# The gates' one-hot products of an expert layer in the rounded format, with the weight split in two halves side by side

## The reference

```python
sc, idx = lax.top_k(s, PEER_TOPK)
cand = (sc[:, :, 0, :, None] + sc[:, :, 1, None, :]).reshape(T, PEER_HEADS, PEER_TOPK * PEER_TOPK)
cidx = (idx[:, :, 0, :, None] * PEER_NKEYS + idx[:, :, 1, None, :]).reshape(T, PEER_HEADS, PEER_TOPK * PEER_TOPK)
top_sc, pos = lax.top_k(cand, PEER_TOPK)
eidx = jnp.take_along_axis(cidx, pos, axis=-1)
gate = jax.nn.softmax(top_sc.astype(jnp.float32), axis=-1).astype(h.dtype)
...
    act = jax.nn.gelu(jnp.einsum('thkd,td->thk', u_tab[eb], hb), approximate=False)
    return jnp.einsum('thk,thkd->td', gb * act, v_tab[eb])
```

## Time and profile before

| | us |
|---|---|
| median of 3 runs | 3858.21 (3856.76 to 3859.42) |
| the profiled execution | 3858.48 |
| its span from first to last instruction | 3856.7 |
| PE busy | 3712.3 (96%) |
| DVE busy | 2270.4 (59%) |
| POOL busy | 1402.2 (36%) |
| ACT busy | 1327.3 (34%) |
| chain that ended last: PE, all lines | 92% |
| of it the gate products, L578 | 3% |
| granted TensorE clock, mean | 0.979 |

### The profile page before, as it was taken

One profiled execution on the slowest core, in us unless ns is written; L12 is line 12 of the kernel. 1 busy time (PEld: TensorE's weight loads), 2 busy tenths in 40 slices (PEclk: granted clock), 3 DMA queues, 4 the chain that ended last, 5 costly groups with the idle time before them and its releaser, 6 DMA issues.

```text
span 3856.7 us, 48588 instructions
## 1 busy us (share of the span) xinstructions
PE 3712.3 (96%) x16460; PEld 2917.3 (76%) x16460; DVE 2270.4 (59%) x3639; ACT 1327.3 (34%) x1826; POOL 1402.2 (36%) x596
## 2 busy tenths in 40 slices
PE   6999899899999999999999999999999999999998
PEld 4787787688888888878888887854688877358886
DVE  5786996145767585167777775335574431657441
ACT  4554323334443434321111113246322232653221
POOL 2211443333333333344444443410244444124442
PEclk8999999999999999999999999989999999899999
DMA  5435222233546464676556652221132223212232
GB/s 200 148 109 195 95 92 78 88 94 111 177 146 188 136 191 134 213 250 187 183 183 186 187 180 95 94 66 43 55 98 93 98 89 96 64 43 93 96 96 77
DMA packets 266641, 486.58 MB, mean 126 GB/s; under 512 B 16721, under 2 KB 148177, under 8 KB 266097
## 3 DMA queue, kind: packets, MB, share of 16 engines
q1 hardware_dynamic: 81936, 299.93, 24.6%
q10 hardware_dynamic: 184580, 184.95, 14.8%
HBM read 415.48 MB, written 84.02 MB: 130 GB/s over the span
## 4 chain that ended last, share of the span: by engine, by line
PE 92%; DVE 3%; ACT 2%; issue 1%; DMA 1%; POOL 0%; DVEq 0%; SPq 0%; ACTq 0%; POOLq 0%
PE ps L356 26%; PE ps L358 26%; PE ps L357 26%; PE ps L578 3%; PE ps L653 3%; PE ps L671 2%; DMA ring<-panels 1%; PE ps L661 1%; PE ps L453 1%; PE ps L389 1%; PE ps L558 0%; PE ps L384 0%; DVE sq L1368 0%; DVE arena L1468 0%; PE ps L464 0%
## 5 line engine op out<-in xcount | busy, mean ns | idle before, releaser
L1967 POOL TENSOR_TENSOR ring_r<-ring,high_w 128x1024 fp32r<-128x1024 f32 x552 | 1366.0, 2476 | 2240.3 <-ACT high_w L770 1757.6
L356 PE MATMUL ps<-uT_r,high_w 128*128 128x512 f32 x2624 | 1047.9, 399 | 23.2 <-POOL ring_r L1967 10.2
L358 PE MATMUL ps<-uT_r,ring_r 128*128 128x512 f32 x2624 | 1028.2, 392 | 0.0
L770 ACT ACTIVATE high_w<-ring 128x1024 fp32r<-128x1024 f32 x440 | 464.4, 1058 | 1283.4 <-PE ps L358 1134.4
L357 PE MATMUL ps<-sq_r,high_w 128*128 128x512 f32 x2048 | 800.0, 391 | 0.0
L357 PE MATMUL ps<-part,high_w 128*128 128x512 f32 x1856 | 735.0, 396 | 0.0
L356 PE MATMUL ps<-part,high_w 128*128 128x512 f32 x1664 | 670.1, 403 | 11.6 <-issue 7.1
L358 PE MATMUL ps<-part,ring_r 128*128 128x512 f32 x1664 | 658.6, 396 | 0.0
L356 PEld LDWEIGHTS ps<-uT_r,high_w 128*128 128x128 f32 x2624 | 497.6, 190 | 131.3 <-issue 19.9
L358 PEld LDWEIGHTS ps<-uT_r,ring_r 128*128 128x128 f32 x2624 | 496.6, 189 | 104.8
L357 PEld LDWEIGHTS ps<-sq_r,high_w 128*128 128x128 f32 x2048 | 386.7, 189 | 79.8 <-issue 1.9
(11 more groups left out here) (288 smaller groups left out, 3770.5 us busy)
## 6 DMA issues: line engine op xcount, KB each, us to landing
ring<-panels SPq DMA_DIRECT2D x568, 512.0 KB, 3.5
gdram<-arena ACTq DMA_DIRECT2D x16, 2048.0 KB, 10.6
arena<-gdram ACTq DMA_DIRECT2D x128, 256.0 KB, 5.3
arena<-adram ACTq DMA_DIRECT2D x128, 256.0 KB, 2.7
adram<-act_out ACTq DMA_DIRECT2D x112, 256.0 KB, 3.9
arena<-ada_rest ACTq DMA_DIRECT2D x32, 512.0 KB, 4.5
strips_dram<-btab ACTq DMA_DIRECT2D x4, 3584.0 KB
arena<-strips_dram ACTq DMA_DIRECT2D x32, 448.0 KB, 3.3
```

The source lines that it names most:

```text
L356: t_.matmul(out, wh, xh, start=(k == 0), stop=False)
L358: last = t_.matmul(out, wl, xh, start=False, stop=(k == KT - 1))
L770: s_.activation(high_w[:, j % RING], ring[:, j % RING], ACT.Copy).then_inc(hi_ready, 1)
L1967: g_.tensor_tensor(ring_r[:, j], ring[:, j], high_w[:, j], ALU.subtract).then_inc(lo_ready, 1)
```

## The change

The four products of a group go to the rounded format. A one-hot is exact in it, the weight is not, so the weight is cut into a high half (rounded) and a low half (what is left). The moving operand then is, per token, two blocks of 128 columns: onehot(a) x high and onehot(a) x low. The product has 256 columns and yields two partial gates, and their sum is the gate. The pieces:

- after L569, DVE copies the transposed keys from PSUM into `slot` in SBUF (L1732 of the changed kernel) and forms the two halves of the weight in `slotT` (L1733, L1734), once per token tile;
- `hot`: one comparison of 1024 elements writes the one-hots of both keys of four tokens (`hots`, in `st`, L1741), one multiplication of 1024 elements writes the two halves (`halves`, in the work area's tile `rest`, L1742). All their inputs are in SBUF;
- PE: four products of 256 columns instead of four plain ones of 128, into two banks per group, 4 to 7 in turn;
- ACT copies the high partial gates into `gbuf` as before, 512 elements;
- `gate_sum`: DVE adds the low partial gates from PSUM to `gbuf`, in place (L1750), 512 elements with the same 512-byte step;
- PE waits for that sum (`g_sum`) where it waited for ACT's copy (`g_evac`), and ahead of the transposes of the next tile. DVE writes the one-hots of two groups ahead of the loop, and then alternates `hot` of the next round with `gate_sum` of this one.

```diff
                 pe.wait_ge(slot_ready, 3 * (tt + 1))
+                pe.wait_ge(g_sum, 32 * tt + 2)
...
                             pe.wait_ge(hot_ready, n * 1 + 1)
-                            pe.wait_ge(g_evac, n * 1 + 1)
+                            pe.wait_ge(g_sum, n * 1 + 1)
                             for k in range(4):
-                                last = t_.matmul(ps[:, 6 + par, k * P:(k + 1) * P], brng[:, 4 * par + k, :],
-                                                 arng[:, 4 * par + k, :], start=True, stop=True)
+                                last = t_.matmul(ps[:, 4 + 2 * par + k // 2, 2 * P * (k % 2):2 * P * (k % 2 + 1)],
+                                                 hots[:, par, 1, k, :], halves[:, par, k], start=True, stop=True)
...
-                                          ps[:, 6 + par, :].rearrange("p (a b) -> p a b", a=4), ACT.Copy).then_inc(g_evac, 1)
+                                          gate_halves(par)[:, :, 0, :], ACT.Copy).then_inc(g_evac, 1)
...
-                with S.loop(16, 4) as i:
+                S.mark(v_.tensor_copy(slot[:, 0:2, :], slotP[:, 0:2, :]))
+                S.done(v_.tensor_scalar(slotT_r[:, 0, :], slotP[:, 2, :], 1.0, None, ALU.mult))
+                S.done(v_.tensor_tensor(slotT_r[:, 1, :], slotP[:, 2, :], slotT_r[:, 0, :], ALU.subtract))
+
+                def hot(i, par):
+
+                    ve.wait_ge(gmm_done, i * 2 + (tt * 32 + par + 1))
+                    at = bass.ds(i * 8 + 4 * par, 4)
+                    keys = iota.unsqueeze(1).unsqueeze(1).broadcast_to([P, 2, 4, P])
+                    S.done(v_.tensor_tensor(hots[:, par], keys, slot[:, 0:2, at].unsqueeze(3).broadcast_to([P, 2, 4, P]), ALU.is_equal))
+                    v_.tensor_tensor(halves[:, par], hots[:, par, 0].unsqueeze(2).broadcast_to([P, 4, 2, P]),
+                                     slotT_r[:, 0:2, at].rearrange("p h t -> p t h").unsqueeze(3).broadcast_to([P, 4, 2, P]),
+                                     ALU.mult).then_inc(hot_ready, 1)
+
+                def gate_sum(i, par):
+
+                    ve.wait_ge(g_evac, i * 2 + (tt * 32 + par + 3))
+                    to = gbuf[:, :, bass.ds(i * 8 + 4 * par, 4)].rearrange("p i t -> p t i")
+                    v_.tensor_tensor(to, gate_halves(par)[:, :, 1, :], to, ALU.add).then_inc(g_sum, 1)
+
+                for par in range(2):
+                    hot(0, par)
+                with S.loop(15, 2) as i:
                     for par in range(2):
-                        ve.wait_ge(gmm_done, i * 2 + (tt * 32 + par + 1))
-                        four = slice(4 * par, 4 * par + 4)
-
-                        def of_slots(n):
-                            return slotP[:, n, bass.ds(i * 8 + 4 * par, 4)].unsqueeze(2).broadcast_to([P, 4, P])
-
-                        keys = iota.unsqueeze(1).broadcast_to([P, 4, P])
-                        S.mark(v_.tensor_tensor(arng[:, four, :], keys, of_slots(0), ALU.is_equal))
-                        S.done(v_.tensor_tensor(brng[:, four, :], keys, of_slots(1), ALU.is_equal))
-                        v_.tensor_tensor(arng[:, four, :], arng[:, four, :], of_slots(2), ALU.mult).then_inc(hot_ready, 1)
+                        hot(i + 1, par)
+                        gate_sum(i, par)
+                for par in range(2):
+                    gate_sum(15, par)
```

More of the change, by code:

```diff
@@ L146, in build @@
         sq, sq_r = both("sq", [P, KT, T])
-        st = sb("st", [P, 4, T])
+        st, st_r = both("st", [P, 4, T])
         ms, sr, rt, rstd = (st[:, n, :] for n in range(4))
@@ L162, in build @@
         part_x = sb("part_x", [P, KT, T], F32R)
-        sb("rest", [P, 27520 - 20000 - KT * T])
+        rest_r = sb("rest", [P, 27520 - 20000 - KT * T], F32R)
         ident, iota = cst[:, 0:P], cst[:, P:2 * P]
@@ L215, in build @@
         srep = view(26624, P)
-        arng = st[:, 0:2, :].rearrange("p a (b c) -> p (a b) c", c=P)
-        brng = st[:, 2:4, :].rearrange("p a (b c) -> p (a b) c", c=P)
+        hots = st_r[:].rearrange("p (a s) (b c) -> p a s b c", a=2, c=P)
+        halves = rest_r[:, 480:2528].rearrange("p (a b h c) -> p a b h c", a=2, b=4, h=2)
         tk = 26752
@@ L227, in build @@
         slot = sb("slot", [P, 3, SLOTS])
-        slotT = sb("slotT", [P, 3, P])
+        slotT, slotT_r = both("slotT", [P, 3, P])
         gsum = sb("gsum", [P, PEER_HEADS, 2])
@@ L286, in build @@
             "hot_ready", "gmm_done", "g_evac", "g_out"))
+        g_sum = sem("g_sum")
         a_out = sem("a_out")
@@ L306, in build, with gate_halves @@
         block = ctx.enter_context(nc.Block())
+        def gate_halves(par):
+            return ps[:, 4 + 2 * par:6 + 2 * par, :].rearrange("p a (b h c) -> p (a b) h c", h=2, c=P)
         def col(name, k=0):
@@ L585, in _ @@
                     panel(i + (2 * Q_PEER + PER_TILE * TT), j, (uT_r, sq_r), unit=4)
-            pe.wait_ge(g_evac, 130)
+            pe.wait_ge(g_sum, 130)
             def up(q, r=None):
@@ L1066, in _ @@
                             s_.activation(gbuf[:, :, bass.ds(c * 32 + (8 * j + 4 * par), 4)].rearrange("p i t -> p t i"),
-                                          ps[:, 6 + par, :].rearrange("p (a b) -> p a b", a=4), ACT.Copy).then_inc(g_evac, 1)
+                                          gate_halves(par)[:, :, 0, :], ACT.Copy).then_inc(g_evac, 1)
                         early(tt * PER_TILE + c + 3, j)
-                act.wait_ge(g_evac, tt * 32 + 34)
+                act.wait_ge(g_sum, tt * 32 + 34)
             def gates(g, par):
@@ L1952, in _ @@
         def _(po):
-            for s in (v_free, og_ready, gmm_done, g_evac, att[0]["pt_ready"], att[1]["pt_ready"], att[0]["o_ready"]):
+            for s in (v_free, og_ready, gmm_done, g_evac, g_sum, att[0]["pt_ready"], att[1]["pt_ready"], att[0]["o_ready"]):
                 po.sem_inc(s, 2)
```

## The result

The changed kernel takes 3993.8 us (median of four runs, 3979.9 to 3995.9) against 3858.8 us of the kernel before (3856.8 to 3860.0): 1.035 times as long, with a 95% interval of 1.0332 to 1.0367. It is slower, by 135 us, where 84 were forecast. The profiled execution's span is 3994.1 us at a mean granted clock of 0.960; before it was 3856.7 us and 0.979.

The account below looks back on a forecast made before the run. PE's own work was taken to bound the kernel before, DVE's round of 8.45 us the changed one. Rounds +73, heads +8 and ends +3 us on 3858.5 gave 3942 us; own range 3895 to 3985, stated range 3885 to 4040.

Parts of the forecast that it names:

- the lock: Each gate-stage round: DVE operations with two SBUF inputs and POOL's operation exclude each other; DVE loses 1.33 us.
- the clock rival: Gate loop: PE's waits bring the clock down, 1 us more in every round, 4002 us; chance 0.18 for 3985 to 4040.
- PE: Gate products: eight rounded 256-column products at 0.115 us, 0.92 us; PE's round falls to 6.46 us, 0.78 less.
- DVE's work: Gate-stage round: two groups of comparison, multiplication and sum with their gaps take 7.12 us (6.02 to 8.22).
- The clock: Gate loop: PE stands 2.0 us a round, between waits of 1.93 and 2.22 us; no time added to the sum.
- Heads: Start of each of four gate stages: DVE's copies and two groups of one-hots delay PE 2 us each, 8 in all.
- Ends: End of a stage, three times: PE waits 1 us for DVE's next slots, 3 us in all.
- DVE fits beside PE: Gate rounds: DVE pays no step and POOL falls beside the sums; PE's 6.46 us set the round, 3819 us; faster 0.09.
- The lock costs nothing: Gate rounds: only the 512-byte step costs, 7.12 us a round, 3862 us; chance of no change 0.05.
- Weights load slowly: Gate products at 0.23 us each: PE's round 7.38 us, still under DVE's; 3942 us stays; no separate chance given.
- sums at 0.69 us: Low end of the forecast's own range: DVE's sum doesn't pay for the step, a round of 7.9 us, 3895 us.
- sums at 1.79 us: DVE's sum pays the step for read and write each: 3985 us, or up to 4090 us with the clock falling.

Follow-up runs that it names:

- two accumulating products: Kernel before, with rounded format, one-hots and halves each reading one PSUM input, two accumulating 128-column products per token and no DVE sum: 3867.8 us, ratio 1.0031.
- half panels: Changed kernel with each gate-stage panel cut in two, 12 products behind each group of a round: 3964.0 us, ratio 1.0279.
- the lock taken away in two different ways: Changed kernel with slots and weight halves kept in PSUM, 3874.4 us; changed kernel with POOL's gate-stage subtraction replaced by a memset, 3881.4 us.

## Why the prediction was right in sign and too small

The sign, the range (3885 to 4040) and the mechanism held: DVE became the bound, through the lock. The predicted time was 52 us too low. The measured 3994 us is above the 3985 at which the forecast's own range ended: the stated range holds it only because it takes in the clock rival up to 4040. By its own steps:

*PE, right.* 0.115 us for a rounded product of 256 columns. Four of them stand 0.47 us before the next work (992.67 to 993.14, above), 0.118 each, and PE's round measured 6.45 against 6.46 us. The reason that I gave for the value, half the columns and half the time, was weak: at 128 columns with a new 128 x 128 load each, a product still takes 0.108 us, as the two accumulating products show.

*DVE's work, mis-sized: 7.12, measured 7.46.* The one-hots took 1.22 us as forecast from the line between 512 and 2048 elements. The sum took 1.34 instead of 1.24 (the step costs 0.66 us on DVE, where ACT's 0.55 of the earlier trace rows was the stand-in): 0.2 a round. And the multiplication starts 0.12 to 0.14 us behind the comparison (1.21 long from 979.03, next at 980.38), not 0.04: I had taken the gap from the earlier trace rows, which stand outside such a loop; the earlier trace rows had it in this very loop, 0.14 us from L1736's end at 965.02 to L1737 at 965.16. That is 0.18 more. The two together, 0.38, are slightly more than the 0.34 measured; over 60 rounds the 0.34 is 20 us.

*The lock, nearly right: 1.33, measured 1.45.* 8.91 us in the kernel with half panels less 7.46 without the lock. In the changed kernel itself DVE is busy for 8.64 us of a round and stands some 0.27 us in its own gaps, which gives 1.45 us too. The bound of 1.24 to 2.4 was right. I had put POOL's start at the end of the second group, where it would fall beside a sum each time; in the trace it does so only in every other round. The rounds alternate between about 1.0 and 2.0 us (the two rows at 1001.13 and 1011.11).

*The clock, at nothing in the sum, measured 0.3 to 0.4.* Here the forecast chose wrongly between itself and its rival. The working had PE standing 2.0 us per round and left the clock at 1.00, since 2.0 lay between 1.93 (no fall) and 2.22 (fall) of the earlier trace rows. But a longer DVE round is a longer wait: 8.91 less 6.46 us would be 2.45 us on average. And the waits aren't equal. Between the two groups of a round PE stands 2.97 us and 0 to 0.2 us in turn in the first stage; that this follows the lock's alternation is my reading, no run tests it. Behind each of those waits of 2.97 us the clock falls. Nor do two rows like the earlier trace rows bound the fall: 2.79 us left the clock at 1.00 and 1.89 us was followed by 0.56 in the third stage (above), and the kernel with half panels had waits of 2.15 to 2.21 us in each stage, nearly all followed by products at full pace. The rival's price, 1 us a round, was too high: the low level behind a long wait costs PE 1.6 or 2.9 us, but DVE is the slower engine and loses only 0.4 us a round. That the rival's 4002 us lies close to 3994 is luck: it is 1 us a round on top of 8.45, where the runs show 0.3 to 0.4 on top of 8.9. The term had a chance of 0.18 and should have been tied to the others: sum, lock and wait are not independent.

The round together: 7.46 + 1.45 + 0.40 = 9.31 us in the first stage, and 9.22 on the average of the four, against 8.45. Over 60 rounds the 0.77 us are 46 us. But 60 x (9.22 - 7.24) = 119 us is more than the rounds really cost. In the kernel before, too, the clock is low behind the wait at the head of a stage (0.50 in 902.46 to 905.46), and its first panel ended 3.0, 2.7, 1.0 and 1.7 us late in the four stages. Its 60 rounds took 443 us and not 60 x 7.24 = 434. I had said that this loss stays as it is; in the changed kernel it is part of the 553 us that the 60 rounds take, since DVE sets them. So the rounds cost 553 - 443 = 110 us, where 73 were forecast.

The account of the profiled executions (3994.1 against 3856.7 us, 137 us): rounds 110, heads 18, ends 2, and 6 outside the four stages, 1.8 ahead of the first transposes and 4.6 behind the last group. The last six no run explains; they are within the spread of the changed kernel's own runs (16 us).

*Heads, too small: 8, measured 18.* PE waits 31.6 us at the first groups of the four stages, against 12.9 us in the kernel before. From the transposes to the second group it is 8.5, 10.7, 10.7 and 8.7 us, against 5.0 to 5.1 each. I had written that a POOL operation falls in between "now and then". It does each time: ACT's rounding of the next weights (L1049) releases POOL just as DVE begins. In the second and third stages two POOL operations fall in, and the second comparison is held as well (3.38 us). In the changed kernel:

```profile
900.97 3.12 POOL L1989 TENSOR_TENSOR ring_r<-ring,high_w 128x1024 fp32r<-128x1024 f32 x1 [2.41 <-ACT high_w L1049]
901.92 3.25 DVE L1742 TENSOR_TENSOR rest<-st_r,slotT_r 128x1024 fp32r<-128x1024 f32 x1
...
905.22 1.23 PE L584 MATMUL ps<-rest,st_r 128*128 128x256 f32 x4 [5.58 <-DVE rest L1742]
```

*Ends, right.* PE waits 3.2 us in all, 1.6 at two of the three and nothing at the third, against 3.

*The rivals.* "DVE fits beside PE" fell: the one-hots are held, as rows 5 said. "The lock costs nothing" would have been 3862 us; with the lock taken away in two different ways the kernel stands at 3874 and 3881. "Weights load slowly", 0.23 us a product, fell: 0.118 us at 256 columns, and 0.108 at 128.

*Two ends of the working that its own terms don't give.* With sums at 0.69 us and a round of 7.9 us the sum is 3858.5 + 0.66 x 60 + 11 = 3909, not 3895. With sums at 1.79 us, 1.33 us of lock and 1 us for the clock it is 8.22 + 1.33 + 1 = 10.55 us a round, 4068, not 4090. Neither touches the forecast of 3942.

What stays open: the exact share of the clock in the 135 us. Half panels and added products each gave back 30 us by the medians and 27 and 22 us by the ratios. Both also shorten PE's waits at the heads, since PE has work there between a stage's first two groups (22.3 and 23.1 us instead of 31.6). So the clock's part lies between some 15 us, DVE's waits for PE alone, and 30. Open too is what decides between 1.00 and 0.5 behind waits of 1.8 to 2.8 us.

## What to carry to other kernels

Before two operations of DVE are joined into one, look at where each operand lives: an operation that loses its PSUM input starts to exclude POOL, and it is POOL's operation, not DVE's, that sets the loss, unless something with a PSUM input stands beside it. A row of an operation far above its line's median, by just one operation of the other engine, is how that looks in a profile.

When the bound moves to an engine that hands back to TensorE, recompute TensorE's waits with the new round, as each single wait and not as a mean. Where they come near 2 us, give the low clock a term of its own in the sum, with a range down to nothing: one harmless wait of 1.93 us in the old trace was no bound, since 1.89 us was followed by 0.56 here. And a saving on TensorE that costs a pass over the result is worth as much as the place that is found for that pass: with nothing held, the kernel with the sum on DVE was 19 us slower than the one before, and with the sum on POOL 35 us faster.

## What the runs showed of the hardware

- **Below 256 columns a rounded product gets hardly shorter.** Sixteen rounded products of 128 columns leave the round at 7.24 us, as eight plain ones of 128 columns do; eight rounded ones of 256 columns bring it to 6.45. With a new 128 x 128 load for each, a rounded product takes 0.11 to 0.12 us at 128 or 256 columns. The Trainium skill, page "TensorE: Matmul & The Clock Gate", section on LDWEIGHTS (loading the stationary operand), has the load cost by the columns of the weights alone, for 128 of them an estimate of 0.107 us; the rounds here agree with 0.11 to 0.12.
- **The lock needs reads on both sides.** A memset of POOL, 0.95 us, lay across two DVE operations with both inputs in SBUF and held neither; a subtraction with two SBUF inputs held such operations, and none with an input in PSUM.
- **A step of 512 bytes costs by engine.** DVE 0.66 us for 512 elements read and written (1.342 against 0.683), ACT 0.5 us for them written (L1072 at 1.09 against 0.60 us). On POOL a sum of 512 elements with the step took 1.61 us; without it no run has it.
- **The length of one wait doesn't tell the clock behind it.** In the third stage of the changed kernel 2.79 us was followed by 1.00 and 1.89 us by 0.56.
- **More work on TensorE made the kernel faster.** 384 products of 0.23 us each, put where the engine stood, brought the clock between 905 and 1040 us from 0.85 to 0.99 and the time from 3994 to 3964 us.
